# Tap slice ahead, masks first, inputs over 128 rows, and the state-space output from stationary states

## The reference, cut to what matters

```python
def rwkv7_recurrence(r, decay, k, v, a_vec, b_vec):
    def step(state, inp):
        r_t, w_t, k_t, v_t, a_t, b_t = inp
        sa = jnp.einsum('bhij,bhj->bhi', state, a_t)
        state = (state * w_t[:, :, None, :] + sa[..., :, None] * b_t[..., None, :]
                 + v_t[..., :, None] * k_t[..., None, :])
        return state, jnp.einsum('bhij,bhj->bhi', state, r_t)
...
def s5_mix(u, ...):
...
    bu_re = jnp.einsum('bsgc,gpc->sbgp', uf, bb_re)
    bu_im = jnp.einsum('bsgc,gpc->sbgp', uf, bb_im)
    _, _, x_re, x_im = lax.associative_scan(complex_affine_combine, (ar_seq, ai_seq, bu_re, bu_im), axis=0)
    y = (jnp.einsum('sbgp,gcp->bsgc', x_re, c_re.astype(f32))
         - jnp.einsum('sbgp,gcp->bsgc', x_im, c_im.astype(f32)))
    y = y.reshape(bsz, s, D_S5) + d_skip.astype(f32) * uf.reshape(bsz, s, D_S5)
    y = jax.nn.gelu(y)
    y = y * jax.nn.sigmoid(y @ glu_w.astype(f32) + glu_b.astype(f32))
    return rmsnorm(y, out_g).astype(u.dtype)
```

## Time and profile before

| what | value |
|---|---|
| median of three runs | 3702.02 us (3690.36 to 3705.0) |
| the profiled execution's own time | 3695.12 us |
| its span, first to last instruction | 3693.4 us |
| mean granted TensorE clock | 0.987 |
| TensorE busy | 3578.4 us, 97% of the span |
| VectorE, ScalarE, GpSimd busy | 2989.7, 1373.7, 728.7 us |
| layer 0: `mixer_tail` begins on TensorE | 404.49 us |
| layer 1: `mixer_tail` begins on TensorE | 2165.84 us |

### The profile page before, as it was taken

The page is one execution under the profiler, slowest core; times in us unless marked ns, Lnnn a source line. Parts: engine busy times, 40 slices in busy tenths (PEclk is TensorE's granted clock), DMA queues, the critical chain, the costliest instruction groups (busy, mean ns, idle before and its releaser), DMA issues. The chain is left out here.

```text
span 3693.4 us, 68447 instructions
## 1 busy us (share of the span) xinstructions
PE 3578.4 (97%) x27950; PEld 3304.6 (89%) x27950; DVE 2989.7 (81%) x5483; ACT 1373.7 (37%) x2082; POOL 728.7 (20%) x592
## 2 busy tenths in 40 slices
PE   8899899999999999999999989999999999999998
PEld 5678777899999999999996877789999999999998
DVE  8677484899998988878886748489999998887887
ACT  3532243433334443333343224343333444333333
POOL 2000000022221123334310000002222212434541
PEclk9999899999999999999999999999999999999999
DMA  7821222488887899999952022248888789999995
GB/s 235 296 69 59 77 103 66 128 286 265 261 258 261 301 348 370 358 351 378 354 202 74 15 111 78 77 130 285 258 260 266 256 305 346 366 358 355 361 362 203
DMA packets 323801, 876.20 MB, mean 237 GB/s; under 512 B 29696, under 2 KB 158848, under 8 KB 315680
## 3 DMA queue, kind: packets, MB, share of 16 engines
q1 hardware_dynamic: 249760, 603.36, 47.7%
q0 software_dynamic: 73728, 268.47, 19.8%
HBM read 746.93 MB, written 124.78 MB: 236 GB/s over the span
## 5 line engine op out<-in xcount | busy, mean ns | idle before, releaser
L2434 POOL DMA_INDIRECT row<-in_peer_u_rows,row_at x256 | 325.1, 1270 | 1663.5 <-DVE row L2708 993.4
L228 PE MATMUL peer_ps<-peer_h_high,tile_high 128*128 128x384 f32 (+1 forms) x1504 | 511.2, 340 | 0.4 <-DVE tile_low L221 0.4
L230 PE MATMUL peer_ps<-peer_h_high,tile_low 128*128 128x384 f32 (+1 forms) x1504 | 508.4, 338 | 0.0
L229 PE MATMUL peer_ps<-peer_h_low,tile_high 128*128 128x384 f32 (+1 forms) x1504 | 508.2, 338 | 0.0
L221 DVE TENSOR_TENSOR tile_low<-peer_tile,tile_high 128x1024 fp32r<-128x1024 f32 x362 | 441.7, 1222 | 62.0 <-ACT tile_high L216 59.0
L228 PE MATMUL peer_ps<-gate_high,tile_high 128*128 128x384 f32 x1360 | 457.7, 337 | 3.2 <-DVE tile_low L221 3.2
L230 PE MATMUL peer_ps<-gate_high,tile_low 128*128 128x384 f32 x1360 | 457.0, 336 | 0.0
L229 PE MATMUL peer_ps<-gate_low,tile_high 128*128 128x384 f32 x1360 | 457.0, 336 | 0.0
L216 ACT ACTIVATE gate_high<-weighed 128x384 fp32r<-128x384 f32 x256 | 134.8, 527 | 681.2 <-PE peer_ps L230 354.9
L216 ACT ACTIVATE tile_high<-peer_tile 128x1024 fp32r<-128x1024 f32 x362 | 379.6, 1049 | 12.4 <-DMA peer_tile<-in_peer_u 12.4
L2567 ACT ACTIVATE up_act<-peer_ps 128x384 f32<-128x384 f32 x240 | 118.1, 492 | 689.7 <-PE peer_ps L230 608.9
(11 more groups left out here) (539 smaller groups left out, 8039.3 us busy)
## 6 DMA issues: line engine op xcount, KB each, us to landing
peer_tile<-in_peer_u SPq DMA_DIRECT2D x256, 512.0 KB, 5.0
peer_tile<-in_peer_v SPq DMA_DIRECT2D x256, 512.0 KB, 6.7
gates<-gates_out SPq DMA_DIRECT2D x24, 2048.0 KB, 12.0
gates_in<-gates SPq DMA_DIRECT2D x32, 1536.0 KB, 11.4
acts<-up_act SPq DMA_DIRECT2D x240, 192.0 KB, 5.3
act_in<-acts SPq DMA_DIRECT2D x240, 192.0 KB, 7.0
in_w<-in_w_in SPq DMA_DIRECT2D x32, 512.0 KB, 3.5
peer_tile<-in_peer_wq SPq DMA_DIRECT2D x32, 512.0 KB, 4.0
```

Source lines behind the costliest of these rows:

```text
L228: pe.matmul(out, wh, mh, start=first, stop=False)
L229: pe.matmul(out, wh, ml, start=False, stop=False)
L230: return pe.matmul(out, wl, mh, start=False, stop=last)
L2434: pool.indirect_dma_start(row_of(n)[:, :], None, table, bass.IndirectOffsetOnAxis(ap=row_at[:, n % ROWS:n % ROWS + 1], axis=0)) \
```

## The change

Four edits, in `mixer`, `rwkv_chunks` and `mixer_tail`:

- **Tap slice ahead.** The taps of tile 1 are loaded at the start of `rwkv_chunks` into `wag`; the other three slices at the start of `mixer_tail`.
- **Masks first.** All four L887 come before the first L889; each raises the count that L809 waits for. L889 and L890 move into level 1, ahead of each seat's L895.
- **Inputs over 128 rows.** A pair has 32 input channels; those of four of a step's 8 tokens are laid on 128 rows (`u_by_step`, by 16 transfers from SBUF to SBUF), so that two products cover a step; the weights are loaded to match by 32 transfers. 64 products of 128x128 weights and 64 columns replace 256 of 32x128 weights.
- **Output from stationary states.** The states become the weights (64x64) and the packed map the moving operand, 128 columns (`map_states`), into the banks `at_front`, steps on the partitions. ScalarE copies them to `pad`, in the order step x channel (`pad_states`), and products with an identity of 64 columns turn them back into `yps` (`turn_back`). The map is loaded in one transfer, and `widen` goes. VectorE does L1297 right behind `x_made`, and L1302 and L1306 behind the splits for the gate; the sum over squares moves behind tile 6.

```diff
-                e_in = [m[n][:, :, :].rearrange("p t n -> p (t n)").rearrange("p (a k n) -> p a k n", a=2, n=P)
+                e_in = [m[n][:, :, :].rearrange("p t n -> p (t n)").rearrange("p (g a n) -> p g a n", g=4, a=2)
                         for n in ("kk", "lw", "cum", "v")]
                 taps = m["ar"][:, :, :, :, :].rearrange("p t b a n -> p (t b a n)").rearrange("p (t k n) -> p t k n", t=4, n=P)
-                rwkv_chunks(pg, layer, r, st, e_in, taps)
+                u_by_step = m["rk"][:, 1].rearrange("p t n -> p (t n)").rearrange("p (t g n) -> p t g n", t=KH, g=4)
+                first_taps = m["wag"][:, :, :].rearrange("p a n -> p (a n)").rearrange("p (k n) -> p k n", n=P)
+                rwkv_chunks(pg, layer, r, st, e_in, first_taps, mixT[:, KH:KD, :], u_by_step)
...
+            sp.dma_start(first_taps, pg.dram["s5_taps"][layer][:, 1]).then_inc(taps_loaded.sem, 16)
             for s in range(SEATS):
                 sp.wait_ge(done[s].sem, done[s].at((ROUNDS - 1) * BATCHES + LOW))
+            for j in range(4):
+                rows = slice(32 * j, 32 * j + 32)
+                for g in range(4):
+                    sp.dma_start(u_by_step[rows, :, g, :], uT[32 * g:32 * g + 32, :, j * P:(j + 1) * P]).then_inc(in_loaded[0].sem, 16)
             for t in range(4):
-                sp.dma_start(e_in[t], pg.dram["s5_e_in"][layer, t]).then_inc(in_loaded[t].sem, 16)
-            for s in range(SEATS):
-                sp.wait_ge(v_taken[s].sem, v_taken[s].at((ROUNDS - 1) * V_BATCHES + V_ENDS))
-            sp.dma_start(taps, pg.dram["s5_taps"][layer]).then_inc(taps_loaded.sem, 16)
+                by_step = pg.dram["s5_e_in"][layer, t].rearrange("(g r) a (j b) n -> j r g a (b n)", g=4, j=4)
+                for j in range(4):
+                    rows = slice(32 * j, 32 * j + 32)
+                    for a in range(2):
+                        sp.dma_start(e_in[t][rows, :, a, :], by_step[j][:, :, a]).then_inc(in_loaded[t].sem, 16)
...
-                    link(dve.tensor_tensor(low[s][:, :, :].rearrange("p (h q) n -> p h (q n)", h=2), ps[s][:, :, 0:2 * CH],
-                                           c["lower_mask"][:, :].rearrange("p (h n) -> p h n", h=1).to_broadcast([P, 2, 2 * CH]), ALU.mult))
-                    link(dve.tensor_tensor(inv[s][:, 1, :, :], low[s][:, :, :], four(c["level0_lower"][:, :]), ALU.mult))
-                    dve.tensor_tensor(inv[s][:, 1, :, :], inv[s][:, 1, :, :], four(c["chunk_ident"][:, :]), ALU.add) \
+                    dve.tensor_tensor(low[s][:, :, :].rearrange("p (h q) n -> p h (q n)", h=2), ps[s][:, :, 0:2 * CH],
+                                      c["lower_mask"][:, :].rearrange("p (h n) -> p h n", h=1).to_broadcast([P, 2, 2 * CH]), ALU.mult) \
                         .then_inc(v_taken[s].sem, 1)
                 for lv in range(1, LEVELS + 1):
                     for s in range(SEATS):
+                        if lv == 1:
+                            dve.wait_ge(v_taken[s].sem, v_taken[s].at(rnd * V_BATCHES + V_LOW))
+                            link(dve.tensor_tensor(inv[s][:, 1, :, :], low[s][:, :, :], four(c["level0_lower"][:, :]), ALU.mult))
+                            dve.tensor_tensor(inv[s][:, 1, :, :], inv[s][:, 1, :, :], four(c["chunk_ident"][:, :]), ALU.add)
...
+IN_LOADS = (16 * 24, 16 * 8, 16 * 8, 16 * 8)
...
-        out_map = [st["both"][:, :, :, :, :].rearrange("p a c t n -> p (a c t n)").rearrange("p (k q c) -> p k q c", k=SC, c=32),
-                   buf("s5_map", [P, SC, S5_PAIRS, 32])]
-        packed = [m["wag"][:, :, :].rearrange("p a n -> p (a n)").rearrange("p (k q c) -> p k q c", k=SC // 2, c=16),
-                  buf("s5_map_packed", [P, SC // 2, S5_PAIRS, 16])]
+        out_map = buf("s5_map", [P, 2, SC, S5_PAIRS, 16])
+        pad = [m["wag"][:, :, :].rearrange("p a n -> p (a n)").rearrange("p (k n) -> p k n", n=P), buf("s5_y_pad", [P, SC, P])]
...
+            sp.wait_ge(taps_loaded.sem, taps_loaded.at(16))
+            sp.dma_start(taps[:, 2:4], dram["s5_taps"][layer][:, 2:4]).then_inc(taps_loaded.sem, 16)
+            sp.dma_start(taps[:, 0], dram["s5_taps"][layer][:, 0]).then_inc(taps_loaded.sem, 16)
             sp.dma_start(turns[:, :, :, :], dram["s5_turns"][layer]).then_inc(turns_loaded.sem, 16)
-            for n in range(len(MAP_PIECES)):
-                part, k0 = MAP_PIECES[n]
-                if n >= 2:
-                    sp.wait_ge(map_made.sem, map_made.at(n - 1))
-                sp.dma_start(packed[n % 2][:, :, :, :], dram["s5_g"][layer][:, part, k0:k0 + SC // 2]).then_inc(map_loaded[n % 2].sem, 16)
+            sp.dma_start(out_map[:, :, :, :, :], dram["s5_g"][layer]).then_inc(map_loaded.sem, 16)
...
-            pool.memset(x[:, :, :, 0:1], 0.0).then_inc(cleared.sem, 1)
+            pool.memset(x[:, :, :, 0:1], 0.0)
+            pool.memset(pad[1][:, :, :], 0.0)
+            pool.wait_ge(moved.sem, moved.at(2))
+            pool.memset(pad[0], 0.0).then_inc(cleared.sem, 1)
...
-                    pe.matmul(yps[t][:, k:SC, :], taps[:, t, k, :], u8[:, t, 0:SC - k, :],
+                    pe.matmul(yps[t][:, k:SC, :], first_taps[:, k, :] if t == 1 else taps[:, t, k, :], u8[:, t, 0:SC - k, :],
...
-                    t, part, k = j // (2 * SC), j // SC % 2, j % SC
-                    if part == k == 0:
-                        pe.wait_ge(in_loaded[t].sem, in_loaded[t].at(16))
-                    for g in range(4):
-                        rows = slice(32 * g, 32 * g + 32)
-                        bank = in_ps[g][:, t * P:(t + 1) * P].rearrange("p (a n) -> p a n", a=2)
-                        last = pe.matmul(bank[:, part, :], e_in[t][rows, part, k, :], u8[rows, t, k, :],
-                                         start=(k == 0), stop=(k == SC - 1))
+                    t, g, part = j // 8, j // 2 % 4, j % 2
+                    if g == part == 0:
+                        pe.wait_ge(in_loaded[t].sem, in_loaded[t].at(IN_LOADS[t]))
+                    bank = in_ps[g][:, t * P:(t + 1) * P].rearrange("p (a n) -> p a n", a=2)
+                    for b in range(2):
+                        last = pe.matmul(bank[:, part, :], e_in[t][:, g, part, b * P:(b + 1) * P], u_by_step[:, t, g, b * SN:(b + 1) * SN],
+                                         start=(b == 0), stop=(b == 1))
                 return last
 
-            groups, each = 4 * 2 * SC, -(-4 * 2 * SC // (NCH - 3))
+            groups, each = 4 * 4 * 2, -(-4 * 4 * 2 // (NCH - 3))
...
+            pe.wait_ge(taps_loaded.sem, taps_loaded.at(48))
...
-            pe.wait_ge(map_made.sem, map_made.at(len(MAP_PIECES)))
+            def map_states(t):
+                pe.wait_ge(spread_taken.sem, spread_taken.at(t + 1))
+                for g in range(4):
+                    q = 4 * t + g
+                    for part in range(2):
+                        for h, hs in halves:
+                            last = pe.matmul(at_front[t][hs, g * P:(g + 1) * P], x[hs, part, q, 0:SN], out_map[hs, part, :, q, :],
+                                             start=part == 0, stop=part == 1)
+                last.then_inc(mapped.sem, 1)
+
+            def turn_back(t):
+                pe.wait_ge(padded.sem, padded.at(t + 1))
+                for k in range(SC):
+                    last = pe.matmul(yps[t][:, k, :], pad[t % 2][:, k, :], pg.c["chunk_ident"][:, :], start=False, stop=True,
+                                     skip_group_check=True)
+                last.then_inc(y_in.sem, 1)
+
+            pe.wait_ge(map_loaded.sem, map_loaded.at(16))
             pe.wait_ge(x_made.sem, x_made.at(1))
             pe.wait_ge(cleared.sem, cleared.at(1))
-            for t in range(KH):
-                for k in range(SC):
-                    for part in range(2):
-                        for g in range(4):
-                            q, rows = 4 * t + g, slice(32 * g, 32 * g + 32)
-                            last = pe.matmul(yps[t][rows, k, :], out_map[part][:, k, q, :], x[:, part, q, 0:SN],
-                                             start=False, stop=part == 1, skip_group_check=True)
-                last.then_inc(y_in.sem, 1)
+            for t in range(KH + 1):
+                if t < KH:
+                    map_states(t)
+                if t:
+                    turn_back(t - 1)
...
-                if j == 5:
+                if j == 6:
...
-            def widen(n):
-                part, k0 = MAP_PIECES[n]
-                act.wait_ge(map_loaded[n % 2].sem, map_loaded[n % 2].at(16 * (n // 2 + 1)))
+            def pad_states(t):
+                act.wait_ge(mapped.sem, mapped.at(t + 1))
+                if t == 0:
+                    act.wait_ge(cleared.sem, cleared.at(1))
+                if t >= 2:
+                    act.wait_ge(y_in.sem, y_in.at(t - 1))
                 for h in range(2):
-                    last = act.activation(out_map[part][:, k0:k0 + SC // 2, :, 16 * h:16 * h + 16], packed[n % 2][:, :, :, :], ACT.Copy,
```

(43 more changed lines are left out.)

13 lines of the change are left out of this document (6 added, 7 removed).

## The result

The changed kernel takes 3679.0 us (median of 6 runs, 3672.6 to 3683.0); the kernel before, in the same comparison, 3698.8 (6 runs, 3690.4 to 3705.0). The ratio is 0.9945 with a 95% interval of 0.9926 to 0.9963, so it is faster by 20 us, give or take 7. The prediction was 3677, range 3662 to 3698. The profiled execution took 3673.7 us. One run of e10 (3965 us) and two of the kernel before (4467 and 12605 us) lie far above all others and are left out of the ranges and ratios of this document.

The account below looks back on a forecast made before the run. TensorE, busy 97% of the span, was taken as the bound. 10.0 + 2 x (6.9 + 2.0 - 0.9 - 0.5) = 25.0 us off 3695.1 gives 3670.1, or 3677 on the median's scale; range 3662 to 3698.

Parts of the forecast that it names:

- The sum: Whole kernel: gains from masks, taps and inputs, less output and margin losses over two layers, total 25.0 us.
- Masks first: Chunk stage: level 2 starts 1.9 us sooner per round in layer 1, 3.3 and 2.9 in layer 0; 10.0 us.
- Taps ahead: Start of mixer_tail: the 6.4 us wait for the taps goes and the clock rises earlier; 6.9 us a layer.
- TensorE's clock falls: Rival, chance 0.07: clock falls in the half-streamed new input sums and turn_back, 14 us a layer, 3705 us.
- Gain 2.0: Input sums: 128 records at 0.107 us plus five state steps take 16.8 us against 18.7; 2.0 us a layer.
- 15 records of 2 columns: Evidence for the input record price: these took 1.60 us at full clock, 0.107 each, so weight load is the floor.
- The tap group of 256 down to 64 columns: Evidence for the same record price: its 1.31 us fits 0.213 + 0.160 + 0.107 + 0.107, twice, and 0.14 latency.
- the walk: Output queues followed from x_made: maps and turns end at 484.1, gate tiles at 495.4 against 494.53; loss 0.9 us a layer.
- The thin margin: Behind the gate: normalised halves and low(10) come barely before they are wanted; 0.5 us a layer added as loss.
- Load and stream add up: Rival, chance 0.06: weight load and streaming add up in the new 128-row records, +20.4 us in all, 3697 us.
- the small transfers come late: Rival, chance 0.05: the 48 input transfers run one after another and TensorE waits in the input sums, 3742 us.
- handed back behind the gate: Rival, chance 0.12: the later sum over squares makes TensorE wait at tile 10 or 11, 4 us a layer, 3684 us.

Follow-up runs that it names:

- e10: Kernel before with masks first and the new input products and transfers, taps late, old output: 3689.4 us, ratio 0.9971 to the kernel before.
- e9: Kernel before with only the new input products and their transfers: 3699.2 us, ratio 1.0000 to the kernel before.
- e2: Kernel before with only the masks first: 3684.8 us, ratio 0.9969 to the kernel before.
- e4: Changed kernel with the whole output edit undone (old product, widening and order): 3673.8 us, ratio 0.9934 to the kernel before.
- e1: Kernel before with only the first tap slice ahead: 3697.9 us, ratio 1.0003 to the kernel before.
- e3: Changed kernel with the input products and transfers of before: 3704.9 us, ratio 1.0020 to the kernel before.
- e6: Kernel before with the tap slice ahead and the masks first, old inputs and output: 3692.4 us, ratio 0.9990 to the kernel before.
- e8: Kernel before with taps ahead, masks first and the new VectorE and ScalarE order behind the old output product: 3689.9 us, ratio 0.9981 to the kernel before.
- e12: Kernel before, unedited, for a second profile: that execution took 5972 us at a mean clock of 0.554.
- e5: Changed kernel with the old output product but the new VectorE and ScalarE order behind it: 3675.1 us, ratio 0.9948 to the kernel before.
- e7: Changed kernel with other widths in the input sums and turn_back, altering part of the computation; 16 turn_back records took 1.88, 1.92 and 1.89 us at 2, 64, 128 columns.
- e11: Changed kernel with the old input products and four later tap products put between their groups: 3679.9 us, ratio 0.9947 to the kernel before.

## Why the prediction was right, and where it was not

*The sum* came near (19.7 us by the medians for 25.0, and 20.3 in the mixer stages), but two of its terms stand on something that it did not have. By the runs, at the scale of 3699 us: masks 11.5 us (0.9969; predicted 10.0), inputs alone 0 (e9, and e2 to e10; predicted 4.0), taps ahead 14 (e10 to e4; 13.8), output 4 lost, unclear (1.8 lost). These are the steps of one path, from the kernel before over e2, e10 and e4 to the changed one, so they add up to the whole by construction; another order would price them otherwise. That 3679 lies 2 us from the predicted 3677 is partly luck: the kernel before came out 3.3 us lower in this comparison than in its first three runs, and the 13.8 us of the taps arrived only because the input edit kept the clock up, which the prediction did not have in it.

*Masks first*: right in mechanism, and in size where level 2 starts, round by round; some 4.4 us of 5.0 a layer are left at the end of the block.

*Taps ahead*: the wait went and the clock rose earlier, 6.7 to 8.1 us a layer for 6.9. What the prediction missed is a condition. It listed "TensorE's clock falls" for the new products and argued against it from the old ones, which "stayed at 1.00". It is the other way round, and one execution could not show it. With old inputs and the taps ahead the clock fell in all eight stretches profiled (e1, e3, e6, e8, two layers each); with old inputs and the taps late in one of four at full clock (e2, layer 0; not in the kernel before) and in both of e12; with new inputs as they are in the change in none of ten (after, e4, e5, e9, e10). So the taps alone are worth nothing (1.0003), and 14 us beside the new inputs. In the output product the rival came true in part as well: in two of the eight stretches with the new one (e3, e7, e11, after) the clock fell, and the gate came 1.7 us later.

*Inputs over 128 rows*: the step that failed is "Gain 2.0" a layer, worked out from the length of the records. Their work is the same to within 0.8 us, since such a record takes 0.112 us inside a run and 0.117 with the change of work, not 0.107; alone they gain nothing. The 0.107 came from a misreading: the 15 in "15 records of 2 columns" counts every record that touches the window, and in the trace they start 0.112 us apart. The tap group of 256 down to 64 columns fits the sum only by accident: its eighth record starts 1.04 us after the first, its last two, of 64 columns, 0.059 apart, and the last one's own duration makes up the 1.31. The worth of the edit is the clock: it is 21 to 28 us once the taps are ahead (e6 to e4, e3 to after), 16.5 and 21.9 of it in the input sums by the traces.

*The output*: the loss was foreseen, 0.9 us a layer by the walk, 1.8 by this pair of traces. From x_made to the gate it took 15.7 us where the walk had 14.7: turn_back 7.45 for 6.85, the maps 7.4 for 7.2, the start 0.1 later. The 25.1 us of before, with its gaps, was no firm figure either (e4). Beside old inputs the edit looks dearer (e3 is 11 us slower than e6, give or take 8).

*The thin margin*: from the gate to the end of the stage 0.5 us are lost in each layer (16.7 us ahead at the gate tiles' end in layer 0, 16.2 at the next stage; 23.4 and 22.9 in layer 1), as put down, though no wait shows that it is this. *Load and stream add up*, *the small transfers come late* and *handed back behind the gate* did not happen: input sums without a wait on a transfer, no stop at tiles 8 to 11.

*What the clock fell with.* One thing stands in the traces that no theory of the experiments named. The 14 stretches of old input products at full clock part without an exception by their longest instruction gap:

| old inputs | stretches | gap in the input sums, us | clock |
|---|---|---|---|
| taps late | before, both layers; e2, layer 1 | 0.35, none, none | 1.00 |
| taps late | e2, layer 0 | 1.22 | fell |
| taps ahead | e1, e3, e6, e8, both layers each | 0.97, 1.72, 1.40, 0.81, 0.72, 1.89, 0.97, 0.99 | fell |
| taps ahead, tap products between | e11, both layers | none, 0.16 | 1.00 |

In each of the nine the clock fell while the gap lasted or at most 2.3 us after it. The gaps are waits for the program itself: each ends 1.2 to 1.6 us after a 16 KB packet has landed in the queue that the profile's page calls "instruction" (here e1's: packets, MB, share), and they stand 256 instructions of TensorE (records and weight loads) apart, or a multiple of it.

```profile
q8 instruction: 220, 3.60, 0.4%
```

The old input sums are 1024 such instructions in 18 us, the new ones 256 in the same time, and there no gap came. So the new inputs may keep the clock because they are wider work, or because they need a quarter of the instructions.

*Left open.* Shown is that the old products in one piece with the taps ahead lose the clock (eight of eight), and that wide products between them (e11) or the new form (ten of ten) keep it. Not shown is by which of the two, since both also take the gap away. The gap alone is not enough: in the old output product gaps of up to 2.6 us passed at 1.00 (e10, layer 0). It is not needed either: in e7 the clock fell without one, behind a thinner stream, and in e12 from its lower level. Why the gap comes with the taps ahead is open too; that the transfers which now run beside the input sums hold the program's packets back is a guess (DMA share 0.52 and 0.44 from 415 to 425 in e1, 0.19 in the earlier trace rows). Whether the output edit costs anything is not settled. No version tried beats the changed kernel by more than the intervals; e4, without the output edit, has the lowest median.

## What to carry to other kernels

Before a gain from a removed wait is counted, look at what the tensor engine does right behind it. Here it was small products over part of the rows, for which the program ran short once for 0.7 to 1.9 us, and which then ran to their end at half the clock. Put wide products between them, or make them full-height and fewer; both gave 21 to 28 us here for the same work. Before you name what held the clock, compare the gaps of the stretches as well as their products. And undo parts one by one: two edits that are worth 0 alone (1.0003 and 1.0000) were worth 13 us together beside the masks (e2 to e4, give or take 9).

## What the runs showed of the hardware

- A float32 record with 128x128 weights takes 0.117 to 0.12 us at 2, 64 and 128 moving columns (e7), 0.112 from start to start inside a run; with 64x128 weights on alternating halves of the rows, 0.065. Four records with 32x128 weights on the four groups of rows take 0.112 together (kernel before).
- TensorE's clock fell from 2.4 to 1.2 GHz at 421.1 in e1, 1.7 us after an instruction gap of 0.97 us, with the engine busy again, and came back at 445.0, 4 us into the 512-column taps that followed (441.0). In e7 it fell at 409.4 without a gap in the input sums.
- 256 products of 32-column weights in 13 us bring two to four instruction gaps of 0.2 to 2.9 us behind their first start, of another length in each kernel, each ending 1.2 to 1.6 us after a 16 KB packet of the instruction queue has landed; 96 larger ones in their place bring none.
